# A change in the order of one turn's weight loads: up, down, then the gate of the expert two ahead

## The reference, cut to what matters

```
comb = sum(one_hot(eid, N_EXPERTS) * wts, axis=1)
act = silu(einsum('nd,edf->nef', xf, w_gate)) * einsum('nd,edf->nef', xf, w_up)
act = act * comb[..., None]
return einsum('nef,efd->nd', act, w_down)
```

## Time and profile before

| | |
|---|---|
| time, median of 3 runs | 1599.87 us (1597.18, 1599.87, 1603.08) |
| profiled execution, its own time | 1600.59 us |
| profiled execution, span from the first to the last instruction | 1598.70 us |
| TensorE busy | 1470.7 us, 92% of the span |
| mean granted TensorE clock | 0.956 |
| DMA moved | 361.20 MB |
| the stage of the change | from 1055 to 1580 us of the span, 18 turns |

### The profile page before, as it was taken

One profiled execution on the slowest core, in us unless ns is written; L12 is line 12 of the kernel. 1 busy time (PEld: TensorE's weight loads), 2 busy tenths in 40 slices (PEclk: granted clock), 3 DMA queues, 4 the chain that ended last, 5 costly groups with the idle time before them and its releaser, 6 DMA issues. The chain is left out here.

```text
span 1598.7 us, 21805 instructions
## 1 busy us (share of the span) xinstructions
PE 1470.7 (92%) x8104; PEld 848.5 (53%) x8105; DVE 608.2 (38%) x1162; ACT 316.0 (20%) x702; POOL 43.7 (3%) x55
## 2 busy tenths in 40 slices
PE   7999999998999798778999999769999999999994
PEld 4478887777888566544444565523333333333331
DVE  3154333432654365466100303523343333433335
ACT  3001011222333144366000203101001010010102
POOL 0000000003000000000000000000000000000000
PEclk9999999999999699798999999879999999999998
DMA  9254537434530377202844024979987999969981
GB/s 348 105 172 160 198 134 261 148 134 149 195 113 7 119 238 236 67 1 89 297 152 164 1 106 155 410 261 419 421 360 274 421 421 422 410 251 421 421 311 66
DMA packets 108867, 361.20 MB, mean 226 GB/s; under 512 B 16600, under 2 KB 44288, under 8 KB 80482
## 3 DMA queue, kind: packets, MB, share of 16 engines
q1 hardware_dynamic: 104546, 329.63, 54.5%
q0 software_dynamic: 3744, 22.43, 3.8%
q10 hardware_dynamic: 512, 8.26, 1.4%
HBM read 388.83 MB, written 17.05 MB: 254 GB/s over the span
## 5 line engine op out<-in xcount | busy, mean ns | idle before, releaser
L2499 PE MATMUL bank<-ring,hT_e 128*64 x576 | 267.1, 603 | 1.8 <-DVE hT_e L2574 1.8
L2500 PE MATMUL bank<-ring,hT_e 128*64 128x512 f32 x576 | 267.1, 603 | 0.0
L2595 DVE TENSOR_TENSOR x<-x,bank 128x1024 f32<-128x1024 f32 (+1 forms) x108 | 131.5, 1220 | 213.2 <-PE bank L2487 210.1
L2499 PEld LDWEIGHTS bank<-ring,hT_e 128*64 128x64 f32 x576 | 73.8, 137 | 179.5 <-issue 179.4
L2517 PE MATMUL bank<-W,const 128*64 128x512 f32 x576 | 127.6, 595 | 11.6 <-ACT const L2552 11.6
L1855 PE MATMUL bank<-W,mixT 128*128 128x512 f32 x256 | 113.4, 604 | 1.6 <-DVE mixT L2090 1.6
L2487 PE MATMUL bank<-const,own_rows 64*128 64x512 f32 (+1 forms) x408 | 95.3, 632 | 0.0
L2517 PEld LDWEIGHTS bank<-W,const 128*64 128x64 f32 x576 | 41.1, 137 | 84.6 <-issue 84.1
L1855 PEld LDWEIGHTS bank<-W,mixT 128*128 128x128 f32 x256 | 49.1, 193 | 63.5 <-issue 61.4
L2500 PEld LDWEIGHTS bank<-ring,hT_e 128*64 128x64 f32 x576 | 73.7, 137 | 0.0
L2550 ACT ACTIVATE gate<-bank 64x512 f32<-64x512 f32 x18 | 10.6, 588 | 307.6 <-PE bank L2500 307.6
(11 more groups left out here) (425 smaller groups left out, 2029.5 us busy)
## 6 DMA issues: line engine op xcount, KB each, us to landing
ring<-in_w_exp_gate SPq DMA_DIRECT2D x80, 1024.0 KB
ring<-in_w_exp_up SPq DMA_DIRECT2D x72, 1024.0 KB
W<-in_w_exp_down SPq DMA_DIRECT2D x72, 1024.0 KB
raw<-in_w_in SPq DMA_DIRECT2D x10, 2048.0 KB
raw<-in_w_in SPq DMA_DIRECT2D x8, 2096.0 KB
W<-in_w_out SPq DMA_DIRECT2D x3, 4096.0 KB, 13.6
k_in<-in_cache_sel_k SPq DMA_DIRECT2D x64, 128.0 KB
v_in<-in_cache_sel_v SPq DMA_DIRECT2D x64, 128.0 KB, 3.3
```

The lines of the kernel that those rows point to most:

```text
L2499: pe.matmul(GATE[0:NS, :], hT[:, c, :], w_g[:, c, :], start=(c == 0), stop=(c == KC - 1))
L2500: mm = pe.matmul(GATE[UP, :], hT[:, c, :], w_u[:, c, :], start=(c == 0), stop=(c == KC - 1))
L2595: ins = dve.tensor_tensor(x[0:rows, r, cols], x[0:rows, r, cols], src, ALU.add)
```

## The change

Two lines change places in SyncE's loop. Before, a turn's issues went out as up, gate (of the expert two ahead), down; after, as up, down, gate. Semaphores, waits, conditions, buffers and sizes are the same, and no other engine's program is touched.

```diff
@@ -2432,8 +2432,8 @@
                     with sp.Fori(1, n) as turn:
                         e, previous = expert_of(turn), expert_of(turn - 1)
                         load_up(turn, e, previous)
+                        load_down(turn, e, previous)
                         load_gate_ahead(turn)
-                        load_down(turn, e, previous)
                     last = count(sp, 1)
                     for q in range(4):
                         sp.wait_ge(gu_used[q], last)
```

## The result

The changed kernel takes 1602.47 us (median of 20 runs, 1598.91 to 1606.11), the kernel before 1599.18 us (20 runs). The ratio is 1.0023, 95% interval [1.0013, 1.0033]: 3.7 us slower, between 2.1 and 5.3 (the medians differ by 3.3). This is within the range and under the bound of 0.5%, but it is no zero: the interval leaves it out. The forecast of +0.5 us had the right place and sign and was about a seventh of the size.

A forecast was written before the change was run, and what follows sets the result against it. TensorE was taken to set the end, with loads only having to be in time. Span 1598.70 plus 0.5 for the hole and 0 for all else gave 1599.2, own time 1601.1, or 1600.4 on the median; range 1597 to 1605.

The forecast's parts named there:

- the hole at the start of the run of six: DMA runs dry behind iteration 6's fourth up quarter; 1.3 us later (0 to 2.6), costing 0.5 us in turn 11.
- the down quarters' earlier issue: Down transfers no longer queue behind 4 MiB of gates; worth 0 to 0.5 us, taken as 0.
- the gates' later one: Gates issued 10.2 us later, behind the waits for the down product; over 30 us remain before use, cost 0.
- the up issues' 2 us: Next turn's first up quarter issued up to 4.5 us later behind the gates; covered by DMA's queue, cost 0.
- iteration 11's down issues: Sign: these issues, held to 7.74 us by SyncE's full queue in the old order, would be back at 5.7 us.
- rival D: Stall in turn 11 at its upper bound, 2.6 us, then a slower TensorE clock losing 2.4: +5, 1604.9 us; chance 0.03.
- Rival C: New order slows the transfers themselves, 400 instead of 421 GB/s: 13 us together, 1613 us; chance 0.03.
- The mechanism's bounds: Loads hidden both ways before and after the change: -0.5 to +2.6 us, so 1599.4 to 1602.5; chance 0.92.
- DMA's end in the run: Sign: in iterations 6 to 11, DMA would end at 1400 to 1402 instead of 1399.5.
- the periods grow in several turns: Sign against the forecast: down products were to stay 28.83 us apart, turn 11 perhaps up to 2.6 more.
- The rate, its other sign: Forecast wrong if DMA windows from iteration 7 on show less than 421 GB/s.
- The margin: How early turn 11's first up quarter lands before TensorE wants it: 0 to 3.1 us, taken as 1.5.

The follow-up runs named there:

- the experiment with both reliefs: Changed kernel with two gate quarters before the down quarters and two behind, and the gather held past the next gate and up product's first quarter: ratio 0.9997.
- the gap of 4.3 us ahead of the gates: Old order everywhere, with iteration 6's gates alone made to wait for the first quarter of the down product: ratio 1.0012.

## Why the prediction was right, and where it was off

That TensorE sets the end of the kernel before and the loads only have to be in time: right, shown by the experiment with both reliefs. The place: right; the hole at the start of the run of six, paid as late up quarters at its end, was the step named. With the old order in iteration 6 and the new one in all others only 0.1 to 0.2 us of the loss are left, so the costs of 0 for the down quarters' earlier issue, the gates' later one and the up issues' 2 us held that closely. The gates went out at 1229.97, the first up quarter at 1234.46, both within what the forecast had after 1.08 us of shift; the 5.71 us of iteration 11's down issues stand where 7.74 stood; the first run has no stall. The granted clock stayed at 1.00 from 1061.8 to 1587.5, both stalls included, and the product behind each took 0.61 us and the next ones 0.59, so the second half of rival D did not come. Its first half, a stall at the upper bound in turn 11, was passed: 3.3 us, in two turns. Rival C is refuted: 421 GB/s as before over whole turns.

The size was not right, and that the number fell inside the range owes something to luck. The mechanism's bounds of 1599.4 to 1602.5 stood on a median of 1599.87 from three runs; the median of 20 is 1599.18. The 1602.47 measured is just under that bound, but as a difference it is 3.3 to 3.7 us, and the mechanism's own bounds were -0.5 to +2.6. Two of the prediction's signs went against it: DMA's end in the run was forecast at 1400 to 1402 and came at 1399.5 + 3.3 = 1402.8 on the clock of the kernel before, and the forecast was to be wrong "if the periods grow in several turns", and they grew in two. The rate, its other sign, stayed.

Two terms of the sum were mis-sized, both the same way.

*The hole*, taken as 1.3 us with bounds 0 and 2.6, left DMA 2.7 us behind. The gap itself is 2.6 us, as forecast. The lower half of the range came from the gather filling it. The gather did so in the gap of 4.3 us ahead of the gates, but gained next to nothing in the changed kernel: 2.7 us behind with it, 2.5 with it moved away. The upper bound held only the time until the first down issue. Behind that issue DMA moves 252 to 324 GB/s for 7.5 us instead of 421; the forecast took a rate from full queues and used it there. Why the rate is low is open. With the gather moved away the lag is no more than the gap, so the slow stretch goes with a gather that runs beside the first down quarters; that rests on one execution. SyncE did not supply too little: the four down quarters were issued 1.8 us apart, an estimate of 585 GB/s, and when the fourth went out the weight queue had moved about one of them. The Trainium skill, page "DMA: Bandwidth & Descriptors", section Bandwidth, gives 341 GB/s for a single transfer of 1 MB against 425 for one of 16 MB (issued by GpSimd). No run here sets a lone transfer against a large one, and the quarters in the hole were not alone, so this case neither bears it out nor refutes it.

*The margin*, taken as 1.5 us, the middle of 0 to 3.1, measured as good as nothing: the old order in iteration 6 leaves DMA 0.5 us behind and stalls 0.16, and in the changed kernel 2.7 us behind became 3.3 us of time. The work was right that it lies between; choosing the middle was not supported by anything. The unevenness of the engines, seen in the tail of 2.5 us at 175 GB/s, should have been put on the late side. With 3.3 for hole and margin together the sum would have been 1602.0 + 1.9 = 1603.9 for the profiled execution; it was 1602.82. On the median of 20 runs before, 1599.18, it would have been 1602.5, and 1602.47 was measured; as the 3.3 is the measured loss, this checks the base and not the mechanism.

The forecast named turn 11 alone. Turn 10 stalled too, and with the gather moved away only turn 11 stalls. How the gather shares DMA with the weight queue packet by packet was not looked at further.

Left open: why DMA is slow behind the gap, and why 2.7 us of lag cost 3.3. The new order in iteration 6 alone costs 0.4 us more than in all of them by the rhythm; 0.3 of it is already in DMA's lag (3.0 against 2.7), and with one execution each it may be scatter. So may the difference between 3.3 (rhythm) and 3.7 us (times).

## What to carry to other kernels

A stream that needs slightly more time than its consumer keeps its debt: a hole of 2.7 us at the start of a run of six turns came back in full four turns later, so look for the point where the queue runs empty, not for the turn that stalls. When transfers change places, ask what is in the queue while the issuer waits. Where the queue is empty, a wait for a buffer belongs behind issues that need none, and two free 1 MiB transfers ahead of it were enough here; in the iterations with a full queue the order cost nothing that shows. Where the trace gives a margin as 0 to 3 us and nothing picks a point in it, work out the case of 0 too. And when a test is to hold one thing equal, read from its trace whether it did: the gap meant to be 2.6 us was 4.3.

## What the runs showed of the hardware that was not expected

DMA's busy share and its rate part behind the gap: share 1.04 at 295 GB/s and 0.87 at 324, against 1.01 to 1.02 at 413 to 426 in the windows of the kernel before. With one down quarter issued every 1.7 to 1.95 us, more than 421 GB/s could carry, beside a gather, DMA stayed some 30% under that rate.

A lag of DMA, once made, stayed the same within 0.1 us over the 62 MB that followed, in every kernel profiled.
